# Sparse attention: weights turned by a product with a diagonal matrix instead of a transposition of scaled weights

## The reference, cut to what matters

```python
q, k, v, qi, ki, wi = jnp.split(h @ w_in, DSA_SPLITS, axis=-1)
...
top_val, top_idx = lax.top_k(score, topk)
valid = top_val > -jnp.inf
ks = gather(k, top_idx)
vs = gather(v, top_idx)
s = jnp.einsum('bqhd,bqjhd->bhqj', qb, ks).astype(f32)
s = jnp.where(valid[:, None], s, -jnp.inf)
p = jax.nn.softmax(s, axis=-1)
return jnp.einsum('bhqj,bqjhd->bqhd', p.astype(vs.dtype), vs)
```

## Time and profile before

| | |
|---|---|
| median of three runs | 1745.6 us |
| the profiled execution, its own time | 1744.83 us |
| span of its instructions in the profile | 1743.0 us |
| TensorE matmul busy | 1689.9 us, 97% |
| VectorE, ScalarE, GpSimd busy | 914.9, 652.8, 354.9 us |
| granted TensorE clock, mean | 0.991 |
| stage of the change (transposes 0 to values 25) | 1238 to 1309 us |

### The profile page before, as it was taken

The page is one execution under the profiler, slowest core; times in us unless marked ns, Lnnn a source line. Parts: engine busy times, 40 slices in busy tenths (PEclk is TensorE's granted clock), DMA queues, the critical chain, the costliest instruction groups (busy, mean ns, idle before and its releaser), DMA issues.

```text
span 1743.0 us, 32563 instructions
## 1 busy us (share of the span) xinstructions
PE 1689.9 (97%) x14063; PEld 1521.7 (87%) x14063; DVE 914.9 (52%) x1808; ACT 652.8 (37%) x1123; POOL 354.9 (20%) x466
## 2 busy tenths in 40 slices
PE   7999999989999899999999999999999999999997
PEld 3777779779988699999999999799769999999887
DVE  5458873453355645565551114898782555656002
ACT  3455534352155543222222223322773322222223
POOL 0001112002211022222222222343012222222221
PEclk9999999999999999999999999999999999999999
DMA  8531110237963268989888999699306889888996
GB/s 312 198 121 60 50 50 4 74 64 181 225 139 76 50 148 191 183 181 182 185 179 191 195 197 204 152 208 211 74 2 146 183 180 184 183 184 184 197 205 156
DMA packets 81647, 265.37 MB, mean 152 GB/s; under 512 B 11632, under 2 KB 15472, under 8 KB 81376
## 3 DMA queue, kind: packets, MB, share of 16 engines
q0 software_dynamic: 59040, 214.98, 58.2%
q1 hardware_dynamic: 18448, 42.52, 7.2%
q10 hardware_dynamic: 4016, 5.78, 1.2%
HBM read 251.44 MB, written 2.10 MB: 145 GB/s over the span
## 4 chain that ended last, share of the span: by engine, by line
PE 91%; DVE 4%; DMA 2%; ACT 2%; issue 1%; ACTq 0%; SPq 0%; POOL 0%; DVEq 0%
PE banks L669 21%; PE banks L670 21%; PE banks L671 21%; PE banks L2025 4%; PE banks L2027 3%; PE banks L2026 3%; PE banks L2320 3%; PE banks L806 1%; PE banks L737 1%; PE banks L721 1%; PE banks L759 1%; PE banks L844 1%; DMA ring<-in_weights 1%; PE banks L1080 1%; DMA w_lo<-in_weights 1%
## 5 line engine op out<-in xcount | busy, mean ns | idle before, releaser
L669 PE MATMUL banks<-hn_hi,w_hi 128*128 128x264 f32 (+2 forms) x2168 | 624.8, 288 | 4.4 <-DMA w_lo<-in_weights 3.6
L670 PE MATMUL banks<-hn_lo,w_hi 128*128 128x264 f32 (+2 forms) x2168 | 617.2, 285 | 0.0
L671 PE MATMUL banks<-hn_hi,w_lo 128*128 128x264 f32 (+2 forms) x2168 | 616.3, 284 | 0.0
L1217 ACT ACTIVATE w_lo<-w_hi 128x1024 fp32r<-128x1024 f32 x202 | 214.1, 1060 | 719.4 <-DMA w_hi<-in_weights 711.1
L669 PEld LDWEIGHTS banks<-hn_hi,w_hi 128*128 128x128 f32 x2168 | 409.3, 189 | 16.7 <-issue 12.2
L670 PEld LDWEIGHTS banks<-hn_lo,w_hi 128*128 128x128 f32 x2168 | 410.5, 189 | 0.6 <-issue 0.2
L671 PEld LDWEIGHTS banks<-hn_hi,w_lo 128*128 128x128 f32 x2168 | 408.2, 188 | 0.3
L1162 POOL DMA_DIRECT2D w_hi<-in_weights x205 | 113.8, 556 | 879.7 <-PE banks L671 796.6
L1169 POOL DMA_DIRECT2D w_lo<-in_weights x205 | 184.0, 900 | 168.6 <-ACT w_lo L1217 121.2
L669 PE MATMUL banks<-a_hi,w_hi 128*128 128x264 f32 (+1 forms) x506 | 160.7, 318 | 1.6 <-DVE u_in L1766 0.8
L670 PE MATMUL banks<-a_lo,w_hi 128*128 128x264 f32 (+1 forms) x506 | 160.7, 318 | 0.0
(11 more groups left out here) (455 smaller groups left out, 2729.4 us busy)
## 6 DMA issues: line engine op xcount, KB each, us to landing
w_hi<-in_weights POOLq DMA_DIRECT2D x205, 512.0 KB, 5.1
w_lo<-in_weights POOLq DMA_DIRECT2D x205, 512.0 KB, 7.2
ring<-in_weights SPq DMA_DIRECT2D x48, 512.0 KB, 4.4
arena<-arena ACTq DMA_DIRECT2D x64, 66.0 KB, 5.3
arena<-arena SPq DMA_DIRECT2D x64, 66.0 KB, 4.4
arena<-in_gate_w SPq DMA_DIRECT2D x8, 512.0 KB, 3.6
h<-in_xT SPq DMA_DIRECT2D x2, 1024.0 KB, 6.5
arena<-in_alibi SPq DMA_DIRECT2D x1, 1024.0 KB, 6.0
```

Source lines behind the costliest of these rows:

```text
L669: mm(o, w[0][:, j, :], x[0][:, k, lo:hi], start=first, stop=False)
L670: mm(o, w[0][:, j, :], x[1][:, k, lo:hi], start=False, stop=False)
L671: ins_ = mm(o, w[1][:, j, :], x[0][:, k, lo:hi], start=False, stop=last)
L1217: nc.scalar.activation(split_at(n)[1], split_at(n)[0].bitcast(F32), ACT.Copy, scale=-1.0).then_inc(S["w_negated"], 1)
```

## The change

Three things change.

First, the weights are no longer scaled. `normalise` goes. In its place `diagonals(v)` takes the reciprocals and builds, for each map of the unit, a diagonal matrix with the reciprocals on its diagonal: one `tensor_tensor` of the identity, repeated m times, with the reciprocals, where m is 4 for n = 1, 2 for n = 2 and 3, and 1 for the last-query units. `transposes(v)` then is an ordinary float32 matmul: the weights' piece is the stationary operand and the diagonal the moving one, so the result is the piece turned and scaled.

Second, VectorE builds the diagonals a unit ahead: those of unit 0 before its dsa_soft(2), and those of unit v+1 in turn v. They lie in three buffers (two in `sq`, one in `pt`), and from v = 3 on the build waits for `a_tr` of unit v-3, which used the same buffer.

Third, the high copies are placed by `HIGH_AT`: one each in turns 16 to 20, 22 and 25.

```diff
--- before.py
+++ after.py
@@ -294,6 +294,7 @@
     hn_hi = sb("hn_hi", [P, KT, T2], F32R)
     hn_lo = sb("hn_lo", [P, KT, T2], F32R)
     sq = sb("sq", [P, 2, T2])
+    sq_flat = sq.rearrange("p a t -> p (a t)")
     hn_hi_flat, hn_lo_flat = (x.rearrange("p k t -> p (k t)") for x in (hn_hi, hn_lo))
     second = ExitStack()
     arena2 = second.enter_context(nc.sbuf_tensor("arena2", [P, ARENA2], F32))
@@ -365,6 +366,16 @@
     def prob1(j):
         return prob_flat[:, j, :]
 
+    def dsa_scale(v):
+
+        at = v % 3
+        return pt.rearrange("p a b -> p (a b)")[:, 512:1024] if at == 2 else sq_flat[:, 512 * at:512 * at + 512]
+
+    def dsa_scaled(v):
+
+        m = 1 if DSA_UNITS[v][0] is None else 4 if DSA_UNITS[v][1] == 1 else 2
+        return dsa_scale(v)[:, 0:m * P].rearrange("p (m t) -> p m t", m=m), stat[:, v % 4, 8:8 + m].rearrange("p (m o) -> p m o", o=1), [P, m, P]
+
     def dsa_prob(v, c):
 
         return prob_flat[:, v % 4 * 2 + c, :] if v % 4 < 2 else prob_more[:, (v % 4 - 2) * 2 + c, :]
@@ -615,7 +626,7 @@
     def outputs_done(v):
         return len(DA_ITEMS) + v + 1 + sum(x <= v for x in LAST_AT)
 
-    HIGH_UNITS = {(None, 1): (0, 4), **{(p, 3): (p, p + 1) for p in range(4, 7)}}
+    HIGH_AT = {16: 0, 17: 1, 18: 2, 19: 3, 20: 4, 22: 5, 25: 6}
 
     def hn_base(v):
         return KT * v
@@ -729,12 +740,12 @@
                 pe.wait_ge(S["a_pt"], DA_N + v)
                 if p is None:
                     for j, (_, kj) in enumerate(TILES):
-                        last = nc.tensor.transpose(psum[0:kj, 4 + j // 4, j % 4 * P:(j % 4 + 1) * P], dsa_prob(v, 0)[:, j * P:j * P + kj], ident[:, :])
+                        last = mm(psum[0:kj, 4 + j // 4, j % 4 * P:(j % 4 + 1) * P], dsa_prob(v, 0)[:, j * P:j * P + kj], dsa_scale(v)[:, 0:P], start=True, stop=True)
                 else:
                     for part in dsa_maps(v):
-                        for _, c, b, at in part:
+                        for i, c, b, at in part:
                             for j in range(at.start, at.stop, P):
-                                last = nc.tensor.transpose(psum[:, 4 + c, j:j + P], dsa_prob(v, c)[:, j:j + P], ident[:, :])
+                                last = mm(psum[:, 4 + c, j:j + P], dsa_prob(v, c)[:, j:j + P], dsa_scale(v)[:, i * P:(i + 1) * P], start=True, stop=True)
                 last.then_inc(S["a_tr"], 1)
 
             def values(v):
@@ -1376,20 +1387,19 @@
                     w = keys(n) + P * (n == 1)
                     A(pt2[:, v % 2, :, 0:w], psum[:, 4:6, 0:w], ACT.Copy).then_inc(S["a_pt"], 1)
 
-            def high(first, end):
-
-                for p in range(first, end):
-                    act.wait_ge(S["a_o"], outputs_done(max(DSA_UNITS.index((p, 3)), LAST_AT[1])))
-                    A(o_hi[:, p, :], oT[:, p, :], ACT.Copy).then_inc(S["o_hi"], 1)
+            def high(p):
+
+                act.wait_ge(S["a_o"], outputs_done(max(DSA_UNITS.index((p, 3)), LAST_AT[1])))
+                A(o_hi[:, p, :], oT[:, p, :], ACT.Copy).then_inc(S["o_hi"], 1)
 
             N = len(DSA_UNITS)
             for v in range(N):
                 if v + 2 < N:
                     dsa_exps(v + 2)
                 copy(v)
-                if v >= 3 and DSA_UNITS[v - 3] in HIGH_UNITS:
-                    high(*HIGH_UNITS[DSA_UNITS[v - 3]])
-            high(7, 8)
+                if v in HIGH_AT:
+                    high(HIGH_AT[v])
+            high(7)
 
         def ffn(i, v, s_up):
             t = tokens(v + 1)
@@ -1693,15 +1703,13 @@
 
         def dsa_attention():
 
-            def normalise(v):
-                p, n = DSA_UNITS[v]
-                maps = [(0, 0, None, slice(0, T2))] if p is None else [m for part in dsa_maps(v) for m in part]
+            def diagonals(v):
+                out, scale, shape = dsa_scaled(v)
                 ve.wait_ge(S["a_exp"], DA_N + v + 1)
-                st.link(V.reciprocal(stat[:, v % 4, 8:8 + len(maps)], stat[:, v % 4, 4:4 + len(maps)]))
-                for i, c, _, at in maps:
-                    x = dsa_prob(v, c)[:, at]
-                    last = V.tensor_scalar(x, x, stat[:, v % 4, 8 + i:9 + i], None, ALU.mult)
-                last.then_inc(S["a_prob"], 1)
+                st.link(V.reciprocal(stat[:, v % 4, 8:8 + shape[1]], stat[:, v % 4, 4:4 + shape[1]]))
+                if v >= 3:
+                    ve.wait_ge(S["a_tr"], DA_N + v - 2)
+                V.tensor_tensor(out, ident[:, :].rearrange("p (m t) -> p m t", m=1).to_broadcast(shape), scale.to_broadcast(shape), ALU.mult).then_inc(S["a_prob"], 1)
 
             def out(v):
                 p, n = DSA_UNITS[v]
@@ -1724,10 +1732,11 @@
 
             ve.wait_ge(S["sel_spread"], 16 * 7)
             N = len(DSA_UNITS)
+            diagonals(0)
             dsa_soft(2)
             for v in range(N + 2):
-                if v < N:
-                    normalise(v)
+                if v + 1 < N:
+                    diagonals(v + 1)
                 if v + 3 < N:
                     dsa_soft(v + 3)
                 if v - 3 in LAST_AT:
```

## The result

The changed kernel took 1765.45 us, the median of four runs (1763.35 to 1767.07), against 1745.85 us for the kernel before in the runs of that comparison (1745.56 to 1748.15). The ratio is 1.0108, with a 95% interval of 1.0091 to 1.0124: slower by 15.9 to 21.6 us. The forecast was 1761.6 us, with a range of 1755.5 to 1767.5. The profiled execution took 1764.77 us with a span of 1763.0 us, 20.0 us more than that of before.

The account below looks back on a forecast made before the run. TensorE was taken to bound the stage: 19.1 us for dearer products, less 1.35 (beginning), 1.10 (middle) and 0.67 (end), gives +16.0 us on 1744.83, 1760.8; the median lies 0.8 higher, so 1761.6 us, range 1755.5 to 1767.5.

Parts of the forecast that it names:

- The bound: Sparse stage, mid-stage: only TensorE time counts, busy 40.00 of 40 us; VectorE and ScalarE have some 7 us of slack.
- The product: Turning step on TensorE: a float32 product is two records, 0.2225 us against 0.11; 170 of them add 19.1 us.
- The switch between steps: TensorE's step into a turning group: about 0.15 us on top of its records, taken as unchanged by the change.
- the 10.2 to 10.4 named as a sign: Mid-stage chain of waits: three units were to take 10.2 to 10.4 us, where they took 8.03 before.
- The sign for eight products: Mid-stage turning group: eight products were to add about 1.8 us to the chain, where eight transpositions added 1.02.
- The beginning: Turning of units 0 and 1: their 12 products, 1.35 us dearer, are paid by the stall there, -1.35 us.
- The end: Chain over ScalarE from copy(22): unit 23's six products are hidden, units 24 and 25 pay 1.58 us; -0.67 us.
- The middle: TensorE's wait for copy(17) behind four high copies goes with one high copy a turn, -1.10 us.
- The first: Rival, turning step: a product costs no more than a transposition, only stalls count; -1.85 us, 1743.7 us; 4 in 100.
- The second: Rival, VectorE's scaling held more turns than the windows show, 6.8 us come back; +12.3 us, 1757.9 us; 7 in 100.
- The third: Rival, turning step: 192 ns weight loads are not hidden, 0.384 us a product; 46.6 us dearer, 1789 us; 3 in 100.
- VectorE at no cost: Building the diagonals, about 0.69 or 0.42 us a unit, delays nothing: 0 us; 10 us if cover failed every turn.

Follow-up runs that it names:

- the rounded product: Changed kernel with the turning product in one-pass float32r, exponentials and diagonals written in that format; ratio 0.9992 against the kernel before, stage -1.90 us.
- the kernel that transposes: Changed kernel with the turning step a transposition with the identity again, diagonals built but unread; ratio 0.9987 against the kernel before, stage -2.00 us.
- the kernel that scales a unit ahead: Kernel before, still transposing, with weights scaled in place a unit ahead and high copies placed by HIGH_AT; ratio 0.9983, stage -1.99 us.

## Why the prediction was right

The measured median, 1765.45 us, is 3.9 us above the forecast. The stage explains 1.6 us of that (17.57 against 16.0). The rest lies outside the stage, where the two programs are the same, so that the whole time came out inside the range owes something to the range's width.

**The bound.** Right. TensorE is full before and after, and issuing its products twice lengthens the stage by their full price.

**The product.** Right in mechanism and price: two records for one, 0.2229 against 0.109 us.

**The switch between steps, "which stays".** Wrong, and the largest error within the stage. A group that opens with a plain product pays 0.20 us, not 0.15. With 26 groups that is up to 1.3 us which the sum does not have. It explains three units: 2.28 + 3 x 0.05 = 2.43, measured 2.42, so that they took 10.45 us and fell just outside the 10.2 to 10.4 named as a sign. The sign for eight products, about 1.8 us, was too low even by the prediction's own terms: 8 x 0.2225 + 0.15 is 1.93, measured 1.98.

**The beginning.** The 1.35 us that were to be paid by the stall. From the start of scores(2) to that of scores(5), the old kernel takes 6.57 us and the changed one 6.71 (weight loads at 1243.43 and, before, 1240.96). Of 1.45 us (1.35 and two openings), 1.31 went.

**The end.** From copy(22) to the projection, give 8.85 us (1299.96 to the load at 1308.81). The changed kernel's chain at the end:

```profile
1318.18 1.03 ACT arena L1388
1319.21 0.14 issue
1319.35 1.58 PE banks L748 x12
1320.93 1.02 PE banks L770 x16
1321.98 1.59 PE banks L748 x12
1323.60 0.82 ACT arena L1388
```

It takes 10.53 us, +1.68, where 20 products and three openings cost 2.40. So 0.72 us was hidden, forecast 0.67, and in the way that was forecast. The turning of unit 24 starts 3.81 us after copy(22) before (1299.96 to 1303.77) and 3.80 us after it now (1318.18 to 1321.98), so unit 23's six products cost nothing. The view of the chain names TensorE here, since its values end at 1321.95, about 0.1 us after ScalarE's copy(23). That copy ends at 1321.84, and the turning follows 0.14 us behind it as it did before:

```profile
1321.04 0.80 ACT L1388 ACTIVATE arena<-banks 128x768 f32<-128x768 f32 x1
```

ScalarE and TensorE are level at this place, so a dearer product would have shown.

**The middle.** 17.57 - 0.14 - 1.68 leaves 15.75 us for 138 products and 21 openings, which cost 16.6 us. So about 0.8 us was saved where I forecast 1.10. About 0.2 of the difference is in the two last-query groups, which add 1.41 us for ten records and added 0.70 for five. Another 0.2 is the price itself: the measured difference of 0.2229 and 0.109 is 0.0014 us above the 0.1125 of the sum, for each of 138 products. With both, the stall of 1.10 us went as forecast; TensorE is busy for 7.00 of 7 us in the window from 1282.

The sum in the stage: 19.1 + 1.3 - 1.3 - 0.7 - 0.8 = +17.6 us, against a forecast of +16.0.

**Ahead of the stage.** The profiled execution has another 2.3 us there, and this is no effect of the change. In the thirteen traces of the table scores(2) start anywhere from 1231.56 to 1240.40, with the same instructions ahead of them, and kernels with and without diagonals lie on both sides. Part of it seems to go with the granted clock. The latest and the second earliest start, the rounded product and the changed kernel with high copies together, in the windows table from 100 to 480 us:

```profile
100.00:480.00 380.00, 359.93 (x3858) 308.48 (x3857) 217.26 (x471) 155.40 (x297) 52.62 (x61) 0.96 0.35 88
```

```profile
100.00:480.00 380.00, 359.37 (x3903) 308.46 (x3902) 216.12 (x469) 155.48 (x295) 54.24 (x64) 0.98 0.36 92
```

The means are 0.96 and 0.98. That the clock is the cause was not tried, and what else moves it stays open.

**The rivals.** The first, a product at a transposition's price, is refuted by the 320 records, and its 1.85 us of stalls turned up as 2.00 us in the kernel that transposes. Its remark that the kernel is slower from about 0.13 us a product on is too low: by its own 3.5 us, 170 x (0.1415 - 0.11) less 1.85, it is 0.14. The second, that more turns were held by the scaling, is refuted by the kernel that scales a unit ahead: with all the matmuls' waits for VectorE gone, the stage gave 2 us, not 6.8. The third, weight loads that are not hidden, is refuted at its price of 0.384 us by 0.2229 us a product, though each record's load lasts 192 ns. Whether loads that follow one another at 0.11 us set that pace is another question, and open (see the last section).

**VectorE at no cost.** Right. No matmul of the changed kernel waits for the diagonals; its weight loads do for 0.9 us in all, at the beginning and at the end. The builds take 0.42 and 0.69 us as bounded by the earlier trace rows.

## What to carry to other kernels

A plain float32 product that stands in for a transposition doubles its records and its time on TensorE, so it pays only where TensorE waits. Relieving an engine is worth the stalls that it causes and no more: here 4.1 us of idle time could be counted ahead, 2 to 2.5 us of it could be had, and reordering alone had it. Where the effect is below the scatter of whole runs, cut the traces at two marks around the stage and compare those lengths.

## What the runs showed of the hardware

- The step into a group on TensorE costs 0.20 us when a plain float32 product opens it and 0.15 us when a transposition does; at the end of a group a product costs no more than its records.
- A one-record product of 128 columns in the rounded format adds as much as a transposition (1.04 against 1.02 us for eight), although it has half the records of the float32 product. It isn't the moving columns that hold it there: in the output projection of the kernel before, records in the same format with 258 moving columns, each with a weight load of its own, follow one another at 20.00/170 = 0.118 us (columns of the earlier trace rows):

```profile
1310.00:1330.00 20.00, 20.00 (x170) 20.00 (x169) 5.56 (x8) 6.72 (x9) 5.72 (x7) 1.00 0.57 129
```

  What does hold a record of 128 columns at 0.11 us, the weight load ahead of it for one, was not tried.
- VectorE's scaling in place is slowed beside GpSimd. In the kernel before, while GpSimd ran four subtractions in a row, two instructions took 1.85 us; two of the same size took 0.90 when a subtraction ran beside the first of them, and 0.75 with none:

```profile
1246.44 0.75 DVE L1703 TENSOR_SCALAR arena<-arena,stat 128x384 f32<-128x384 f32 x2
...
1293.57 1.31 POOL L1175 TENSOR_TENSOR o_lo<-arena,o_hi 128x528 fp32r<-128x528 f32 x1 [3.81 <-ACT o_hi L1383]
1294.53 0.90 DVE L1703 TENSOR_SCALAR arena<-arena,stat 128x384 f32<-128x384 f32 x2
```

  The diagonals' products are slowed as well. In the changed kernel none of them runs beside a subtraction, and those of 256 elements take 0.42 us. With the high copies together four subtractions stand in a row again, and the one that falls among them takes 0.96:

```profile
1294.25 5.28 POOL L1186 TENSOR_TENSOR o_lo<-arena,o_hi 128x528 fp32r<-128x528 f32 x4 [60.93 <-ACT o_hi L1394]
...
1297.41 0.96 DVE L1713 TENSOR_TENSOR sq<-ident,stat 128x256 f32<-128x256 f32 x1
```
